# Two order changes in one kernel: the second feed-forward's first up-projection for both token tiles at once, and the first attention's normalisation ahead of the next maxima

## The reference, cut to what matters

```
p = jax.nn.softmax(jnp.concatenate([s_loc, s_ctx, sink_col], axis=-1), axis=-1)   # layer 0, 16 heads
...
x = x + mx[2] * rms_norm(y_x, g[1])                                               # layer 1
x = x + mx[5] * rms_norm(sqrelu_mlp(modulate(rms_norm(x, g[2]), mx[3], mx[4]), mlp_w1[i], mlp_w2[i]), g[3])

def sqrelu_mlp(h, w1, w2):
    return jnp.square(jax.nn.relu(h @ w1)) @ w2        # w1 1024x4096, w2 4096x1024
```

## Time and profile before

| | |
|---|---|
| three runs | 1767.89, 1770.12, 1770.85 us (median 1770.12) |
| the profiled execution | 1767.38 us, of which the span from first to last instruction is 1765.6 us |
| mean granted TensorE clock | 0.945 of full speed (2.4 GHz) |
| TensorE busy | 1617.0 us |
| VectorE, ScalarE busy | 1107.0 us, 862.2 us |
| memory traffic | 158 GB/s over the span |

### The profile page before, as it was taken

The page is one execution under the profiler, slowest core; times in us unless marked ns, Lnnn a source line. Parts: engine busy times, 40 slices in busy tenths (PEclk is TensorE's granted clock), DMA queues, the critical chain, the costliest instruction groups (busy, mean ns, idle before and its releaser), DMA issues.

```text
span 1765.6 us, 24431 instructions
## 1 busy us (share of the span) xinstructions
PE 1617.0 (92%) x8850; PEld 1330.8 (75%) x8850; DVE 1107.0 (63%) x1817; ACT 862.2 (49%) x1404; POOL 13.1 (1%) x36
## 2 busy tenths in 40 slices
PE   4999989899999999898779999798888799999999
PEld 3754548888888888777569999696566798978888
DVE  2345663744444456689955666687466578687795
ACT  3234545723333327587744444544333466556573
POOL 2000000000000000000000000000000000000000
PEclk9989999899999999999866999899898799999999
DMA  8377742323333322332423666352221289878792
GB/s 317 102 304 257 254 188 72 116 79 101 97 95 95 95 85 71 96 95 84 128 75 96 186 185 188 108 169 93 84 72 36 71 287 345 296 257 328 275 340 113
DMA packets 195802, 279.72 MB, mean 158 GB/s; under 512 B 12434, under 2 KB 111220, under 8 KB 190588
## 3 DMA queue, kind: packets, MB, share of 16 engines
q1 hardware_dynamic: 194308, 274.21, 46.7%
q0 software_dynamic: 1152, 4.19, 0.6%
q10 hardware_dynamic: 248, 0.09, 0.0%
HBM read 277.40 MB, written 1.05 MB: 158 GB/s over the span
## 4 chain that ended last, share of the span: by engine, by line
PE 73%; DVE 15%; ACT 7%; issue 3%; DMA 1%; SPq 0%; DVEq 0%; ACTq 0%; POOL 0%; POOLq 0%
PE bank L433 63%; DVE weights_lo L406 3%; PE bank L701 2%; ACT weights_hi L394 1%; PE bank L1306 1%; PE bank L1290 1%; DVE work L2636 1%; PE bank L1274 1%; DVE work L2673 1%; DVE work L2683 1%; DMA x_and_ctx<-in_ctx_dram 1%; DVE x_and_ctx L2636 1%; DVE x_and_ctx L553 1%; DVE work L2515 1%; ACT work L543 1%
## 5 line engine op out<-in xcount | busy, mean ns | idle before, releaser
L406 DVE TENSOR_TENSOR weights_lo<-stage,weights_hi 128x1024 fp32r<-128x1024 f32 x332 | 394.3, 1220 | 81.7 <-ACT weights_hi L394 78.1
L394 ACT ACTIVATE weights_hi<-stage 128x1024 fp32r<-128x1024 f32 x332 | 337.8, 1055 | 150.5 <-PE bank L433 102.2
L433 PE MATMUL bank<-act_hi,weights_hi 128*128 128x256 f32 (+2 forms) x1072 | 346.6, 323 | 18.2 <-DVE weights_lo L406 9.6
L433 PE MATMUL bank<-act_lo,weights_hi 128*128 128x256 f32 (+2 forms) x1072 | 344.2, 321 | 0.0
L433 PE MATMUL bank<-act_hi,weights_lo 128*128 128x256 f32 (+2 forms) x1072 | 344.0, 321 | 0.0
L433 PEld LDWEIGHTS bank<-act_hi,weights_hi 128*128 128x128 f32 x1072 | 216.7, 202 | 34.0 <-DVE weights_lo L406 11.3
L433 PEld LDWEIGHTS bank<-act_lo,weights_hi 128*128 128x128 f32 x1072 | 217.0, 202 | 11.2
L433 PEld LDWEIGHTS bank<-act_hi,weights_lo 128*128 128x128 f32 x1072 | 216.7, 202 | 11.1
L433 PE MATMUL bank<-weights_hi,ff_hi 128*128 128x512 f32 x560 | 220.9, 395 | 1.9 <-DVE ff_lo L2850 1.9
L433 PE MATMUL bank<-weights_hi,act_hi 128*128 128x512 f32 (+1 forms) x488 | 197.5, 405 | 25.0 <-DVE act_lo L2697 16.2
L433 PE MATMUL bank<-weights_hi,ff_lo 128*128 128x512 f32 x560 | 220.2, 393 | 0.0
(11 more groups left out here) (395 smaller groups left out, 2057.0 us busy)
## 6 DMA issues: line engine op xcount, KB each, us to landing
stage<-in_mlp_w_dram SPq DMA_DIRECT2D x128, 512.0 KB, 4.0
stage<-in_w_dram SPq DMA_DIRECT2D x96, 512.0 KB, 6.0
ada_rows_in<-in_ada_w_dram SPq DMA_DIRECT2D x40, 1024.0 KB, 5.5
x_and_ctx<-in_w_dram SPq DMA_DIRECT2D x48, 512.0 KB, 6.0
work<-in_w_dram SPq DMA_DIRECT2D x48, 512.0 KB, 6.5
stage<-in_w_in_dram SPq DMA_DIRECT2D x32, 512.0 KB, 4.4
stage<-in_lru_w_in_dram SPq DMA_DIRECT2D x20, 512.0 KB, 4.4
stage<-in_attn_w_qkv_dram SPq DMA_DIRECT2D x12, 512.0 KB, 4.7
```

Source lines behind the costliest of these rows:

```text
L394: act.eng.activation(whi[u % NRING][:], landing(act, u)[:], ACT.Copy).then_inc(sem("hi_ready"), 1)
L406: dve.eng.tensor_tensor(wlo[u % NRING][:], landing(dve, u)[:], whi[u % NRING][:].bitcast(F32), ALU.subtract).then_inc(sem("lo_ready"), 1)
L433: m = pe.eng.matmul(ps, l, r, start=start and j == 0, stop=stop and j == 2, skip_group_check=True)
```

## The change

In the second feed-forward the first group's up-projection is done once, with the 256 columns of both token tiles, behind both turns. TensorE, ScalarE and VectorE get the new order; the splits of the weight units keep their number (ten on each engine) and move with it. In the attention, VectorE's normalisation of half h-1 is put ahead of the maxima of half h.

```
-        FF = {"m0_first": 8, "m0_last": 8, "m1_first": 8, "m1_last": 4}
+        FF = {"m0_first": 8, "m0_last": 8, "m1_first": 4, "m1_last": 4}
...
-                            if n == 0 and 2 * tt % ntt == 0:
+                            if n == 0 and 2 * tt % ntt == 0 and FF[group] >= 4 * half + 4:
...
-            TOK = [slice(0, P), slice(P, TX)]
             turn_pe(pe, "n1b", 0, lambda tt: xn_a[:, tt, :])
-            first_hidden("m1f", "n1b", TOK, lambda: turn_pe(pe, "n1b", 1, lambda tt: xn_a[:, tt, :]))
+            turn_pe(pe, "n1b", 1, lambda tt: xn_a[:, tt, :])
+            u0, hviews = pe.unit, []
+            for m in range(4):
+                hviews.append(unit_begin(pe, (KT, P)))
+                hidden_pe(pe, "m1f", 0, m, hviews, XTOK,
+                          (lambda k: turned_at("n1b", "lo", 1, max(k, 1))) if m == 0 else None, True, u0 + m)
             mlp_first_y_pe(pe, "m1f", "m1_first", 2)
...
             turn_act(act, "n1b", 0, True)
-            split_hi(act, 2)
-            for m in (0, 1):
-                hidden_act(act, "m1_first", m, "m1f", 0, m, slice(0, P))
             turn_act(act, "n1b", 1, True)
-            for m in (2, 3):
-                hidden_act(act, "m1_first", m, "m1f", 0, m, slice(0, P))
-            split_hi(act, 2)
+            split_hi(act, 3)
             for m in range(4):
-                hidden_act(act, "m1_first", 4 + m, "m1f", 1, m, slice(P, TX))
-                split_hi(act, 1)
+                hidden_act(act, "m1_first", m, "m1f", 0, m, slice(0, TX))
+                split_hi(act, 2 if m == 3 else 1)
             split_hi(act, 2)
...
             for h in range(34):
+                if 1 <= h < 33:
+                    g = h - 1
...
+                    v.wait_ge(sem("exps"), g + 1)
...
+                    for i in range(2):
+                        v.tensor_scalar(prob[g % 3][:, i, 0:nk], prob[g % 3][:, i, 0:nk], sm[:, 3, at + i:at + i + 1],
+                                        None, ALU.mult).then_inc(*dve.mark("p_norm"))
                 if h < 32:
...
                 if h - 1 in ADA_TURN:
                     ada_dve(dve, ADA_TURN[h - 1])
-                if 1 <= h < 33:
-                    g = h - 1
...
-                    v.wait_ge(sem("exps"), g + 1)
...
                 if h >= 3 and h % 2:
```

More of the change, by code:

```diff
@@ L2487, in _ @@
             for h in range(34):
+                if 1 <= h < 33:
+                    g = h - 1
+                    nk = P * len(key_tiles(HALVES[g][3]))
+                    at = 2 * (g % 2)
+                    cols2 = slice(at, at + 2)
+                    v.wait_ge(sem("exps"), g + 1)
+                    v.tensor_tensor(sm[:, 3, cols2], sm[:, 1, cols2], sm[:, 2, cols2], ALU.add).then_inc(*dve.mark())
+                    v.wait_ge(*dve.own())
+                    v.reciprocal(sm[:, 3, cols2], sm[:, 3, cols2]).then_inc(*dve.mark())
+                    v.wait_ge(*dve.own())
+                    for i in range(2):
+                        v.tensor_scalar(prob[g % 3][:, i, 0:nk], prob[g % 3][:, i, 0:nk], sm[:, 3, at + i:at + i + 1],
+                                        None, ALU.mult).then_inc(*dve.mark("p_norm"))
                 if h < 32:
@@ L2503, in _ @@
                     ada_dve(dve, ADA_TURN[h - 1])
-                if 1 <= h < 33:
-                    g = h - 1
-                    nk = P * len(key_tiles(HALVES[g][3]))
-                    at = 2 * (g % 2)
-                    cols2 = slice(at, at + 2)
-                    v.wait_ge(sem("exps"), g + 1)
[L2510 to L2516, removed]
                 if h >= 3 and h % 2:
@@ L2728, in _ @@
             turn_dve(dve, "n1b", 0, True)
-            split_lo(dve, 2)
-            for m in (0, 1):
-                hidden_dve(dve, "m1_first", m, m, slice(0, P))
             turn_dve(dve, "n1b", 1, True)
-            for m in (2, 3):
-                hidden_dve(dve, "m1_first", m, m, slice(0, P))
-            split_lo(dve, 2)
+            split_lo(dve, 3)
             for m in range(4):
-                hidden_dve(dve, "m1_first", 4 + m, m, slice(P, TX))
-                split_lo(dve, 1)
+                hidden_dve(dve, "m1_first", m, m, slice(0, TX))
+                split_lo(dve, 2 if m == 3 else 1)
             mlp_first_y_dve(dve, "m1f", 2, Y2, (1, 1))
```

## The result

The changed kernel takes 1738.24 us, the median of 4 runs (1734.56 to 1741.36), against 1769.01 us for the kernel before on the same chip (4 runs, 1764.89 to 1770.85). The ratio is 0.9828, 95% interval 0.9802 to 0.9855: 30.8 us less. The profiled execution took 1734.56 us, its span 1732.8.

A forecast was written before the change was run, and what follows sets the result against it. TensorE, busy 92%, was taken to bound the kernel through matmuls, waits and low-clock streaming. Feed-forward -26.8, attention -6 and low stretch -1 sum to -33.8: 1733.6 from the profiled 1767.4, plus 2.7 for the median, 1736; range 1728 to 1750.

The forecast's parts named there:

- Narrow costs as much as wide at the same clock: Up-projection: at the low clock a 128-column matmul costs 0.2125 us, a 256-column one 0.21; the skill's page gives 106.7 ns for 128.
- The climb of the clock, 4.5 us: Wide up-projection: 4.5 us at the low clock, 21 matmuls, then 75 at 0.12 us; earlier streams took 3.5 or 5.7.
- Rival A: Clock stays low to the end of the up-projection; loop -18.2 us in place of -26.8, time 1745; chance 0.10.
- The loop: Second feed-forward: the loop behind the down-projection starts at 937.05 in place of 963.89, 26.8 us earlier.
- The hidden work: Feed-forward weight splits and fetches, moved later, stay covered with 14 us of slack; costed at nothing.
- rival C: Staging buffers freed 5 us later starve the down-projection or the loop's start; half the gain lost, about 1750; chance 0.05.
- The attention: Transposes' waits for VectorE's normalisation: 14 of 15, 9.1 us, end; about 3 is given back, net -6 us.
- The new chain: Attention: VectorE must wait out ScalarE's exponentials, 8.8 us a pair against TensorE's 8.55; gives back 3 us.
- the low stretch behind the first wait of 1.53 us: Attention modulation step at low clock, 1.94 us: probably goes with the wait ahead of it, between 0 and 1.7, taken as -1.
- Rival B: VectorE and ScalarE's chain bounds the attention, 9.6 us a pair against 9.02, about +9 in place of -7; time 1752; chance 0.08.
- Rival D: Slower than before: the loop is entered at low clock and stays there, 18.6 us more a trip; two trips 1773; chance 0.03.
- The part between: Between the attention and the feed-forward: held unchanged; the prediction is wrong if it grows.

The follow-up runs named there:

- e3: Changed kernel with the up-projection back in two narrow passes of 128 columns behind both turns: 1759.52 us, 0.9947 of the kernel before.
- e4: Changed kernel with units 2 and 3 of the wide up-projection cut into 128-column halves, 96 narrow matmuls for 48 wide: 1742.39 us.
- e8: Changed kernel with up-projection units 1 to 3 in 128-column halves, each streamed twice, 288 narrow matmuls behind 24 wide: 1758.34 us.
- e1: Changed kernel with VectorE's attention loop as before, so the feed-forward part alone: 1739.88 us, 0.9857 of the kernel before.
- e2: Kernel before with only VectorE's attention loop changed: 1761.29 us, 0.9957 of the kernel before.
- e9: Kernel before plus 26 unused 256-column matmuls between the first turn and the first narrow pass: 1767.29 us, 0.9986 of the kernel before.
- e12: Kernel before plus 26 unused 256-column matmuls between the first and second unit of the first narrow pass: 1764.33 us, ratio 0.9980.
- e6: Changed kernel with the two weight splits at attention half 28 taken one at a time over neighbouring halves: 1731.47 us, 0.9794 of the kernel before.
- e7: Changed kernel with one wide turn of both token tiles, eight pairs of 128x256 scalings on ScalarE in place of 32 of 128x128: 1736.40 us.
- e5: Changed kernel with the attention's normalisation ahead of the modulation addition only, still behind the maxima: 1742.75 us, 0.9842 of the kernel before.

## Why the prediction was right

The prediction named 1736, and the median is 1738.2. The sum was made against the profiled execution, 1733.6, and that of the changed kernel took 1734.6. That this is so near is in part luck: the low stretches behind the loop alone move a total by several us. What bears the prediction out are the stretches that the change touches. Point by point:

- **Narrow costs as much as wide at the same clock**, the row against the rule of the Trainium skill's page "TensorE: Matmul & The Clock Gate". Shown at the low clock by the earlier trace rows and e3 (0.2135), and at the full one by e4 and e8 (0.111 against 0.12). Of the 27.3 us by which e3's narrow stream is longer than the wide one, 96 matmuls more at 0.2135 are 20.5; the clock is the other 6.8.
- **The start, 5.5 us later**: 5.6.
- **The climb of the clock, 4.5 us**: 4.8, and 4.7 to 5.3 in the eight other kernels with the wide stream, inside the bounds of 3.5 and 5.7. Rival A would have shown 0.50 at 920.
- **The end of the up-projection**, 20.95 us behind the first scaling: 21.3. **The down-projection**, 10.9: 11.2 here, 10.9 in e1. **The loop**, -26.8: -26.25.
- **The hidden work**: ScalarE did wait for a transfer, and TensorE never did, which ends rival C:

```profile
917.57 1.06 ACT L394 ACTIVATE weights_hi<-stage 128x1024 fp32r<-128x1024 f32 x1 [1.58 <-DMA stage<-in_mlp_w_dram]
```

- **The attention**: 9.1 us of waits end: 9.1 (13.1 to 4.0), and at the weight splits one of 3.6 stays, with two of 0.16 elsewhere. The new chain gives back 3: 2.4 in waits for ScalarE. Net -6 was named, and 6.3 is what the order is worth at the same low time (e1 against e2). The step that doesn't hold is the next one, -1 for the low stretch behind the first wait of 1.53 us: e1 and e9 have that wait and not the stretch, so it is not the wait's alone, and that the profiled execution before had it and the changed kernel's hadn't is chance in part. The sum of both, -7 against -7.7 measured, is so near with some luck. Rival B, the chain as the bound, cost 0.2 to 0.4 at a time.
- **Rival D**, a loop at the low clock: nothing of it. The loop runs at 0.12 a wide matmul from its first.
- **The part between**, held unchanged: it grew by 1.0 us, from 637.1 to 638.1. The program of this part is the same in all kernels, and it took 637.1 to 640.1 us in the fourteen profiled executions, 637.2 in e12 and 639.3 in e9 with everything up to there as before. So 1.0 us is less than it varies with nothing changed ahead of it. The low clock isn't the cause: it was low for 44.6 us of the part before and for 44.7 in the changed kernel. The cause stays open.

What the prediction left open is why the old passes never got their clock; it only noted that 192 matmuls hadn't raised it. e3, e8, e9 and e12 say more: it isn't the turn between the passes, it is the width, together with what stood ahead of the stream and, once the clock is up, the pauses in it.

## What to carry to other kernels

In rounded float32 a matmul of 256 columns cost about what one of 128 did here, at either clock, so look for token tiles that can be merged, even where the first matmul must then wait for both; here the first matmul waited 5.6 us longer for the second tile and the loop still came 26 us earlier. Look at the granted clock of every stretch of narrow or paced matmuls: it tells whether a stream that looks busy runs at half speed. Where an engine does two jobs in a row and another engine waits for the second of them, put the awaited one first, and put weight splits one at a time between halves rather than two together (4.4 us here, e6).

## What the runs showed of the hardware

- An unbroken stream of 128-column matmuls left the clock at 1.2 GHz for 41.0 us (e3), and the same stream kept it at 2.4 GHz for 32.1 us behind 24 wide ones (e8). So the stream alone doesn't say at which clock it will run; what ran ahead of it counts too.
- A narrow stream that came in threes, one three every 0.7 us, lost a full clock 4.1 us behind its first matmul, with no pause in it over 0.4 us (e9). The wide stream gained the clock after 4.7 to 5.3 us in nine kernels; in e7, where its last threes were 0.9 us apart, it was 4.7.
- A 128-column matmul in rounded float32 starts 0.111 us after the last at 2.4 GHz and 0.2135 at 1.2 GHz, about as a 256-column one. That the weight load sets this would fit, since each matmul has one of the same size and PEld is busy throughout in e3 and e8; but it is so in the changed kernel's wide stream too (13.71 of 13.71 us), and no run here separates it.
- The program behind the loop's start, the same in all, took 794.3 us in e2 and 806.1 in e5, the ends of fourteen profiled executions, with 65 and 89 us of it at the low clock.
